# Turning the outer group's tiles of the first norm by DMA in an eight-core diffusion layer

## The chip, the cores and the metric

The kernel runs as one program on the 8 cores of a Trainium2 chip. Each core works on its own 2,048 of the 16,384 latent tokens and no core waits for another in the part that this text is about. The metric is the device time in microseconds of the slowest core.

## The reference, cut to what matters

One layer mixes windowed attention and a gated MLP over tokens, and then runs a feed-forward net. Everything that reads the input reads it through a norm and a modulation:

```
hc = modulate(layer_norm(ctx), mod_c[0], mod_c[1])      # 256 context tokens
kc, vc = context_kv(hc, w_in)
h  = modulate(layer_norm(x), mod_x[0], mod_x[1])        # latent tokens
q, k, v, u, vb, ga, gb = split(h @ w_in)
# window attention: block n reads keys and values of blocks n-1, n, n+1 and all of kc, vc
# modulate(y, shift, scale) = y * (1 + scale) + shift, shift and scale per feature
```

A core's window attention also needs the keys and values of the 128 tokens before and the 128 tokens behind its segment.

## The kernel before

The first norm writes its result with features on the partitions: `hT` holds 8 chunks of 128 features by 2,304 tokens, `hcT` the same for the 256 context tokens. The tokens come in five groups of four tiles of 128 tokens. Groups 0 to 3 are the core's own tokens; group 4, the outer group, is the tile before the segment, the tile behind it, and the two context tiles (columns 2048 to 2303 of `hT`, and all of `hcT`).

For every group the steps are: `ln_stats` (VectorE, L413 to L415), `ln_rstd` (GpSimd and VectorE, L418 to L422), `ln_norm` (ScalarE, L428: the normalised tile `xnh[i]` in bf16), `ln_turn` (TensorE, L442: 8 transposes of 128x128 per tile, into PSUM) and `ln_out` (L459 on ScalarE for chunks 0, 1, 4, 5; L463 on VectorE for chunks 2, 3, 6, 7), which reads the turned chunk from PSUM, applies scale and shift, and writes `hT` or `hcT`.

Every engine has one queue, written out in program order. The order comes from `do(seq, side)`: `seq` is a list of TensorE units (of 8 matmuls each), and `side` maps the number of a unit to work that is put behind that unit. In the stage of this change `seq` is eight units for token group 3, `u_unit` (L528) and `vb_unit` (L558) in turn. Behind a `vb_unit` the norm of the gated MLP is queued too: `vn_stats` (VectorE L570, L571; GpSimd L572, L574), and after the next unit `vn_norm` (VectorE, L581). The side work `s3` holds the norm of group 4, and also `p0_issue` and `p0_compute`: blocks of the modulation weights `wada`, 1 MB each in bf16, are loaded through GpSimd's DMA queue and used by TensorE (L349), whose result VectorE adds to (`mod_out`, L359 and L362). The last two of them, blocks 8 and 9, are `p0_compute(0)` and `p0_compute(1)` behind unit 7; they use banks 0 and 1.

Behind the eight units come, in TensorE's order: `qk_mm(4, 4)` (L488: keys of the outer tiles, bank 2; its matmul k waits for chunk k of `hT`), the context keys (L705, bank 0, which waits for all of group 4 and for what bank 0 held: the `mod_out` of block 8), `v_unit(4)` (L540: 32 matmuls, the values of the four tiles), the matmul of the rotary step (L499), and the first scores of attention (L809), which wait for the rotated keys of the outer tile (VectorE L503 and L505, GpSimd L511). Attention, the merge, the feed-forward net and the last norm follow.

SP's queue carries loads and stores. In the stage it holds the two loads of the rotary tables for group 4 (L240), and behind them nothing until the loads of `wout` at 203 us. Later in the kernel, `c2_turn` (L1039) turns the tiles of the second norm by DMA from SP's queue, and `c2_out` (L1044) modulates them in place by VectorE, 128x512 at a time.

Of the kernel before, what the change touches and what calls it, by code (L numbers as in the profile page):

```python
# [9 lines left out]
ALU = mybir.AluOpType  # L10
# [129 lines left out]
def build_nc(debug_stop=None):  # L140
    nc = bass.Bass("TRN2", target_bir_lowering=False)
    es = ExitStack()
    S = Sched()
# [68 lines left out]
    hT, _, nbA = A.alloc(BF16, [8, TH])  # L212
# [36 lines left out]
    def colpos(ti):  # L249
        return {0: 2048, NT + 1: 2176}.get(ti, (ti - 1) * 128)  # L250
# [6 lines left out]
    hcT, _, nb = A.alloc(BF16, [8, CTX], at=o); o += nb  # L257
# [13 lines left out]
    xnh = [A.alloc(BF16, [D], at=at)[0] for at in (  # L271
        RD + 16 * 1024, RD + 18 * 1024, RE_FREE + 20 * 1024, RE_FREE + 22 * 1024)]
# [5 lines left out]
    groups = [[('x', 1 + 4 * g + i) for i in range(4)] for g in range(4)]  # L278
# [46 lines left out]
    def sp_consts():  # L325
        t_gb.append(sp_load(g1bc, badabc_d[:, 0:1024], 'g1b'))
        t_gb.append(sp_load(g2bc, badabc_d[:, 1024:2048], 'g2b'))
        for dst, src in ((bsbc, bsbc_d), (esink, esink_d), (glgc, glgc_d)):
# [7 lines left out]
                 deps=[t_sc])  # L336
# [29 lines left out]
    def mcol(kind, chunk, which):  # L366
        return modc4[:, kind, chunk, which:which + 1]
# [37 lines left out]
    ln = [dict(ag=[None] * 4, xn=[None] * 4) for _ in groups]  # L405
    xnh_free = [None] * 4
    mv_free = [None] * 4
    t_hT = [[None] * 8 for _ in groups]
# [57 lines left out]
            fb_free[banks[n // 2]] = t_hT[g][c] = t_e  # L466


    qraw_free = [None, None]
    rt_free = [None, None]  # L470
    t_qg = [[] for _ in range(4)]
# [123 lines left out]
    t_mod = [[], []]  # L595
# [46 lines left out]
    def side_of(g, at, last):  # L642
        side = {}

        def put(n, *work):
            side.setdefault(min(n, last), []).extend(work)

        for i in range(4):
            if g < 4:
                put(at + i, (ln_stats, g, i))  # L650
                put(at + 4 + i, (ln_norm, g, i))
            else:
                put(at + i, (ln_norm, g, i))
            n = at + (8 if g < 4 else 4) + i
            if i:
                put(n, (ln_out, g) + PAIRS[i - 1] + (t_mod,))
            put(n, (ln_turn, g) + PAIRS[i])
        if g < 4:
            side[at + 3].append((ln_rstd, g))
        put(n + 1, (ln_out, g) + PAIRS[3] + (t_mod,))  # L660
        return side
# [10 lines left out]
    def add(side, n, *work):  # L672
        side.setdefault(n, []).extend(work)
# [21 lines left out]
        rope_load(g + 2)  # L695


    s3 = side_of(4, 0, 7)
    add(s3, 1, (p0_compute, 1), (p0_issue,))
    add(s3, 7, (p0_compute, 0), (p0_compute, 1))  # L700
    do([x_ for m in range(4) for x_ in ((u_unit, m, 3), (vb_unit, 3, m))], s3)
# [2 lines left out]
    for k in range(8):  # L704
        t_mm = S.op('pe', lambda e, k=k, pq=bk(b_)[:, 0:CTX]: e.matmul(pq, lhsT=wqk[:, 4, k, :], rhs=hcT[:, k, :],  # L705
                                                                     start=(k == 0), stop=(k == 7)),
                    deps=[fb_free[b_], t_hT[4]] if k == 0 else (), sig=(k == 7))
# [432 lines left out]
    for n, (r, tg) in enumerate(order):  # L1140
# [14 lines left out]
        if tg == 3:  # L1155
            if r + NWR < NR:
                load_w1(r + NWR)
            if r == 2:
                for i in range(2, NR):
# [4 lines left out]
                    out=scb2, in_=sc[:, 0:8].unsqueeze(2).to_broadcast([128, 8, 128])), deps=[t_wg2])  # L1164
# [239 lines left out]
```

How the kernel before makes its waits and increments, by code:

```python
            def body(engine, items=items):  # L93
                for (ws, fn, sigkey, inc) in items:
                    for (p, t) in ws:
                        engine.wait_ge(sems[p], t)
                    if fn is None:
                        continue
                    ins = fn(engine)
                    if sigkey is not None:
                        ins.then_inc(sems[sigkey], inc)
```

## Time and profile before

| | us |
|---|---|
| median of 3 runs | 980.13 (980.02 to 981.34) |
| the profiled execution's own time | 986.05 |
| span of its slowest core (core 2) | 984.4 |
| spans of the eight cores | 975.5 to 984.4 |
| TensorE busy on core 2 | 889.6 (90%) |
| VectorE, ScalarE, GpSimd busy | 482.3, 285.5, 239.2 |

The time is that of the slowest core; the profile shows one execution, and its rows are in microseconds from the start of a core's span. What one stage costs is read from the waits inside that stage, not from the busy shares of the whole.

### The profile page before, as it was taken

The numbers are of one execution on the slowest core, as the hardware profiler recorded it, in microseconds if no ns is written. First come the engines' busy times: TensorE is split into PE (matmuls) and PEld (weight loads), VectorE is DVE, ScalarE is ACT, GpSimd is POOL, SyncE is SP. The second block draws the span as 40 slices with busy tenths as digits, with TensorE's granted clock in tenths as the row PEclk, the third lists the DMA queues.
The fourth block names the chain that finished last, engine by engine and source line by source line (L and its number), as shares of the span: only waits on it lengthen the run. The fifth ranks groups of instructions, "written<-read, shape, count | busy, mean of one in ns | idle before, by whom it ended". The sixth has DMA issues, their size and how long they took to land.

```text
span 984.4 us, 15135 instructions; the slowest of 8 cores (975.5 to 984.4 us)
## 1 busy us (share of the span) xinstructions
PE 889.6 (90%) x5195; PEld 427.0 (43%) x5273; DVE 482.3 (49%) x946; ACT 285.5 (29%) x392; POOL 239.2 (24%) x282
## 2 busy tenths in 40 slices
PE   0568898889989999999998999999999999999993
PEld 0324444545544444444443444444444444444442
DVE  2147564466742366567677411122211114777774
ACT  1225545489932223332332311111111110000000
POOL 5024333266632345445443103010000000000000
PEclk9999898999999999999999999999999999999997
DMA  8999785159730023236845139962211004333231
GB/s 168 172 198 207 151 189 75 23 97 180 146 119 1 1 97 108 65 98 151 170 128 107 44 65 156 169 102 43 43 17 27 1 1 150 105 110 122 93 107 45
DMA packets 57964, 99.68 MB, mean 101 GB/s; under 512 B 20896, under 2 KB 21408, under 8 KB 57888
## 3 DMA queue, kind: packets, MB, share of 16 engines
q0 software_dynamic: 21136, 40.44, 26.4%
q1 hardware_dynamic: 36752, 58.25, 19.5%
q8 instruction: 44, 0.72, 0.3%
q14 instruction: 32, 0.26, 0.1%
HBM read 118.14 MB, written 16.78 MB: 137 GB/s over the span
## 4 chain that ended last, share of the span: by engine, by line
PE 71%; DMA 9%; DVE 6%; ACT 6%; issue 4%; POOL 1%; SPq 0%; another core or an unknown queue 0%; DVEq 0%; ACTq 0%; POOLq 0%
PE bank L1073 27%; PE bank L953 15%; PE bank L1204 14%; DMA arena<-wada 7%; ACT arena L812 4%; PE bank L984 4%; PE bank L488 2%; DMA arena<-xh 2%; PE bank L809 1%; PE bank L558 1%; PE bank L528 1%; DVE arena L1028 1%; PE bank L805 1%; PE bank L828 1%; DVE arena L1044 1%
## 5 line engine op out<-in xcount | busy, mean ns | idle before, releaser
L1073 PE MATMUL bank<-arena 128*128 128x512 bf16 x1380 | 303.8, 379 | 4.4 <-DVE arena L1084 1.9
L1073 PEld LDWEIGHTS bank<-arena 128*128 128x128 bf16 x1408 | 137.6, 98 | 169.7 <-issue 4.6
L953 PE MATMUL bank<-arena 128*128 128x512 bf16 x752 | 166.9, 379 | 2.2 <-DVE arena L969 0.9
L1084 DVE TENSOR_TENSOR arena<-bank,arena 128x512 bf16<-128x512 f32 x88 | 60.8, 692 | 217.6 <-PE bank L1073 209.5
L1204 PE MATMUL bank<-arena 128*128 128x512 bf16 (+1 forms) x734 | 151.5, 366 | 0.7
L1082 ACT ACTIVATE arena<-bank 128x512 f32<-128x512 f32 x88 | 52.2, 595 | 219.1 <-PE bank L1073 219.0
L953 PEld LDWEIGHTS bank<-arena 128*128 128x128 bf16 x768 | 74.9, 98 | 92.3 <-issue 2.7
L1204 PEld LDWEIGHTS bank<-arena 128*128 128x128 bf16 x748 | 73.2, 98 | 79.1
L969 DVE TENSOR_TENSOR arena<-bank,arena 128x512 f32<-128x512 f32 x64 | 43.2, 690 | 84.1 <-PE bank L953 65.5
L812 ACT ACTIVATE arena<-bank 128x1024 bf16<-128x1024 f32 x80 | 76.3, 1027 | 4.8 <-PE bank L809 4.5
L962 ACT ACTIVATE arena<-bank 128x512 f32<-128x512 f32 x64 | 36.7, 591 | 101.9 <-PE bank L953 101.9
L1017 ACT ACTIVATE arena<-arena 128x1024 f32<-128x1024 f32 (+1 forms) x32 | 38.5, 1235 | 81.1 <-DVE arena L1015 81.1
L984 PE MATMUL bank<-arena 128*128 128x512 bf16 x252 | 57.6, 379 | 2.7 <-DVE arena L1007 2.5
L971 POOL TENSOR_TENSOR arena<-arena 128x512 bf16<-128x512 f32 x32 | 45.1, 1409 | 57.5 <-DVE arena L969 46.1
L511 POOL TENSOR_TENSOR arena<-arena 128x512 bf16<-128x512 f32 (+1 forms) x21 | 26.0, 1240 | 89.0 <-DVE arena L505 89.0
L243 POOL DMA_DIRECT2D arena<-wff x22 | 16.4, 759 | 128.3 <-PE bank L1073 128.3
L488 PE MATMUL bank<-arena 128*128 128x512 bf16 (+1 forms) x164 | 39.5, 385 | 7.5 <-DMA arena<-wqk 3.0
L1225 ACT ACTIVATE arena<-arena 128x1 f32<-128x1 f32 x16 | 4.7, 294 | 136.3 <-DVE arena L1224 136.3
L1024 POOL TENSOR_TENSOR arena<-arena 128x1024 f32<-128x1024 f32 x16 | 37.7, 2357 | 24.4 <-ACT arena L1017 24.3
L984 PEld LDWEIGHTS bank<-arena 128*128 128x128 bf16 x256 | 24.9, 98 | 33.2 <-issue 3.4
L809 PE MATMUL bank<-arena 64*128 64x512 bf16 x160 | 31.3, 384 | 6.6 <-ACT arena L812 2.9
L442 PE MATMUL bank<-arena 128*128 128x128 bf16 x160 | 13.9, 236 | 25.0 <-ACT arena L428 24.7
(107 smaller groups left out, 869.6 us busy)
## 6 DMA issues: line engine op xcount, KB each, us to landing
arena<-xh SPq DMA_DIRECT2D x34, 512.0 KB, 6.1
arena<-wada POOLq DMA_DIRECT2D x12, 1024.0 KB, 17.2
arena<-wff POOLq DMA_DIRECT2D x11, 1024.0 KB, 10.0
xmid_d<-arena SPq DMA_DIRECT2D x16, 512.0 KB, 2.9
arena<-xmid_d SPq DMA_DIRECT2D x16, 512.0 KB, 3.8
out<-arena SPq DMA_DIRECT2D x32, 256.0 KB, 2.0
arena<-wff POOLq DMA_DIRECT2D x11, 512.0 KB, 20.0
arena<-wout SPq DMA_DIRECT2D x16, 256.0 KB, 4.5
```

Source lines behind the costliest of these rows:

```text
L488: t_mm = S.op('pe', lambda e, k=k, pq=pq, m=m, rhs=hT[:, k, g * 512:g * 512 + n_]: e.matmul(pq, lhsT=wqk[:, m, k, :], rhs=rhs, start=(k == ...
L809: t_mm = S.op('pe', lambda e, psb=bk(2 * i2 + kv), ksrc=ksrc, kv=kv, j=j, first=not masked: e.matmul(psb, lhsT=ksrc[kv * 64:(kv + 1) * 64, ...
L812: t_e = S.op('act', lambda e, pt=PT[slot], psb=bk2(2 * i2): e.activation(out=pt.rearrange('p a b -> p (a b)'), in_=psb, func=AF.Exp, scale ...
L953: t_mm = S.op('pe', lambda e, k=k, n=n, p=bk(bank), lhs=w[:, lo + k, :], rhs=src[:, k, tok]: e.matmul(p, lhsT=lhs, rhs=rhs, start=(k == 0) ...
L969: fb_free[2 + i] = t_p = S.op('dve', lambda e, dst=sga[r + i], p=bk(2 + i): e.tensor_tensor(out=dst, in0=p, in1=dst, op=ALU.mult), deps=[d ...
L971: t_merged[(m, tg)] = S.op('pool', lambda e, dst=merged[tg % 2][:, m, :], a=sga[r], b=sga[r + 1]: e.tensor_tensor(out=dst, in0=a, in1=b, o ...
L984: rhs=woutb[:, k, half * 512:(half + 1) * 512]: e.matmul(p, lhsT=lhs, rhs=rhs, start=(k == 0), stop=(k == 7)),
L1017: st_free[slot] = t2 = S.op('act', lambda e, w=w, dst=dst: e.activation(out=dst, in_=w, func=AF.Identity, scale=mv[:, 2:3], bias=mv[:, 3:4 ...
L1073: rhs=h2T[:, k, tok]: e.matmul(p, lhsT=lhs, rhs=rhs, start=(k == 0), stop=(k == 7)),
L1082: fb_free[b0] = t_s = S.op('act', lambda e, dst=sgb[s_], p=bk(b0): e.activation(out=dst, in_=p, func=AF.Silu), deps=[t_p[0], sg_free[s_]])
L1084: fb_free[b0 + 1] = sg_free[s_] = t_act[(f, tg)] = S.op('dve', lambda e, f=f, p=bk(b0 + 1), sg=sgb[s_]: e.tensor_tensor(out=act[f][:, tok] ...
L1204: t_mm = S.op('pe', lambda e, pd=bk(b_)[:, 0:cs.stop - cs.start], f=f, t=t, cs=cs: e.matmul(pd, lhsT=act[f][:, t * 128:(t + 1) * 128], rhs ...
```

## The change

The outer group no longer goes through `ln_turn` and `ln_out`. Behind each of the first four units `ln_norm` is followed by `ln_dturn`, which puts one DMA transpose of a whole 128x1024 tile on SP's queue. Behind unit 6 `ln_dmod` modulates chunks 0 to 3 in place, behind unit 7 chunks 4 to 7: two VectorE instructions of 128x256 per chunk, one in `hT` (waits for tiles 0 and 1) and one in `hcT` (waits for tiles 2 and 3). Groups 0 to 3 stay as they are.

```diff
+    def ln_dturn(i):
+        kindt, ti = groups[4][i]
+        dst = hT[:, :, colpos(ti):colpos(ti) + 128] if kindt == 'x' else hcT[:, :, ti * 128:(ti + 1) * 128]
+        ln[4][('dt', i)] = S.dma('sp', lambda e, dst=dst, src=xnh[i]: e.dma_start_transpose(out=dst, in_=src),
+                                 'hturn%d' % i, deps=[ln[4]['xn'][i]])
+
+    def ln_dmod(chunks, t_mod):
+        for c in chunks:
+            for h, which, t_d in ((hT[:, c, 2048:2304], 0, [ln[4][('dt', 0)], ln[4][('dt', 1)]]),
+                                  (hcT[:, c, :], 1, [ln[4][('dt', 2)], ln[4][('dt', 3)]])):
+                t_hT[4][c] = S.op('dve', lambda e, h=h, c=c, which=which: e.tensor_scalar(
+                    out=h, in0=h, scalar1=mcol(1, c, which), scalar2=mcol(0, c, which), op0=ALU.mult, op1=ALU.add),
+                    deps=[t_d, t_mod[c // 4]])
...
-    s3 = side_of(4, 0, 7)
+    s3 = {0: [(ln_norm, 4, 0), (ln_dturn, 0)], 1: [(ln_norm, 4, 1), (ln_dturn, 1)], 2: [(ln_norm, 4, 2), (ln_dturn, 2)],
+          3: [(ln_norm, 4, 3), (ln_dturn, 3)], 6: [(ln_dmod, (0, 1, 2, 3), t_mod)], 7: [(ln_dmod, (4, 5, 6, 7), t_mod)]}
     add(s3, 1, (p0_compute, 1), (p0_issue,))
     add(s3, 7, (p0_compute, 0), (p0_compute, 1))
```

## Rows read from the trace of the kernel before

**Rows 1.** Spans and mean granted TensorE clock of two cores.

```profile
core 2: 984.4 us, clock 0.983
core 3: 979.2 us, clock 0.980
```

**Rows 2.** Chain that ended last, core 2 (start, length, what).

```profile
161.00 16.13 DMA arena<-wada
```

**Rows 3.** Timeline of TensorE, core 2 (start, length, line, operands, count, [idle before <-releaser]).

```profile
167.33 0.68 PE L442 MATMUL bank<-arena 128*128 128x128 bf16 x8
167.85 1.89 PE L558 MATMUL bank<-arena 128*128 128x512 bf16 x8
...
177.27 0.99 PE L349 MATMUL bank<-arena 128*128 128x2 bf16 x32 [1.91 <-DMA arena<-wada]
...
179.33 1.91 PE L705 MATMUL bank<-arena 128*128 128x256 bf16 x8
181.03 2.44 PE L540 MATMUL bank<-arena 128*128 128x128 bf16 x32
183.31 0.27 PE L499 MATMUL bank<-arena 128*128 128x256 bf16 x1
185.33 0.39 PE L809 MATMUL bank<-arena 64*128 64x512 bf16 x2 [1.76 <-POOL arena L511]
```

**Rows 4.** Timeline of SP and ScalarE, core 2.

```profile
158.78 1.78 SPq L240 DMA_DIRECT2D arena<-ropes  x1
...
166.36 1.23 ACT L428 ACTIVATE arena<-arena 128x1024 bf16<-128x1024 f32 x1
```

**Rows 5.** All 16 DMA transposes of core 2 (L1039), issue to landing.

```profile
DMA to landing us min/median/max: 2.7/2.8/10.8
```

**Rows 6.** The DMA transpose issued at 455.3 us, core 2.

```profile
L1039 SPq DMA_TRANSPOSE arena<-arena x1: 1238/1238/1238, 455.3 to 455.3; - x1
...
DMA to landing us min/median/max: 10.1/10.1/10.1
```

**Rows 7.** The weight load (L243, wff) issued at 455.1 us, core 2.

```profile
DMA to landing us min/median/max: 10.0/10.0/10.0
```

**Rows 8.** Stretches of core 2 (us, length, granted clock, DMA share, GB/s).

```profile
357.50:358.50 1.00, 1.00 0.95 218
358.50:359.50 1.00, 1.00 0.21 44
...
170.00:177.00 7.00, 1.00 0.75 133
179.00:182.00 3.00, 0.50 0.02 5
```

**Rows 9.** Timeline of VectorE, core 2, in this stage.

```profile
174.88 0.69 DVE L570 BATCH_NORM_STATS2 arena<-arena 128x6 f32<-128x512 f32 x1 [0.34 <-ACT arena L562]
...
175.78 1.37 DVE L463 TENSOR_SCALAR arena<-bank,arena 128x256 bf16<-128x256 bf16 x4
...
178.36 0.17 DVE L359 TENSOR_TENSOR arena<-bank,arena 128x8 f32<-128x8 f32 x1 [0.86 <-PE bank L349]
178.64 0.17 DVE L362 TENSOR_SCALAR arena<-arena 128x8 f32<-128x8 f32 x1
```

**Rows 10.** Timeline of VectorE, core 2, modulation in place of the second norm.

```profile
554.47 2.68 DVE L1044 TENSOR_SCALAR arena<-arena 128x512 bf16<-128x512 bf16 x8
```

**Rows 11.** Timeline of TensorE, core 3.

```profile
172.19 1.84 PE L349 MATMUL bank<-arena 128*128 128x2 bf16 x64
...
175.47 1.03 PE L705 MATMUL bank<-arena 128*128 128x256 bf16 x8
...
180.16 0.39 PE L809 MATMUL bank<-arena 64*128 64x512 bf16 x2 [1.75 <-POOL arena L511]
```

**Rows 12.** The load of wada issued at 159.9 us, core 3.

```profile
L243 POOL DMA_DIRECT2D arena<-wada x1: 1006/1006/1006, 159.9 to 159.9; - x1
...
DMA to landing us min/median/max: 12.8/12.8/12.8
```

## The prediction

> **What bounds the kernel now.** I read the spans of all cores first: 975.5 to 984.4 us, core 2 the longest and core 3 nearer to the middle [rows 1]. The profiled execution took 986.05 us, 1.65 above its longest span and 5.9 above the median of the runs. So I work out a difference inside core 2, test it on core 3, and add it to the median.
>
> The page says that TensorE is busy 90% of the span. In the stage of this change the chain of waits says something else: on core 2 it runs for 16.13 us over a transfer, the load of `wada` block 9, issued at 161.00 and landed at 177.13 [rows 2]. The timeline of TensorE shows the same: it has finished all its units, waits 1.91 us for that load, and goes on at 177.27 [rows 3]. From there it is a serial chain: the keys of the outer tiles, the context keys at 179.33, the values at 181.03, the rotary step, the first scores at 185.33. After that every engine follows TensorE's order, with nothing left that waits for a clock time. So what the first scores lose, the kernel loses. I found no slack behind them that would give it back.
>
> Core 3 has the same chain without the wait: both `wada` blocks run back to back (64 matmuls in 1.84 us), the context keys start at 175.47, the first scores at 180.16 [rows 11], with the load landing at 159.9 + 12.8 = 172.7 [rows 12].
>
> **What the change removes.** 32 transposes leave TensorE. Eight of them move the next unit by 167.85 - 167.33 = 0.52 us [rows 3]; the other three blocks cost 0.45 each, 1.87 in all. On core 2 this makes TensorE wait 1.87 us longer for block 9: worth nothing. On core 3 it would be worth at most what lies between 172.19 + 0.92 (the start of the second block) and 172.7, about 0.4 us. ScalarE loses eight `ln_out` instructions, but the rest of them sits behind TensorE's units, and on core 2 nothing after them is due before block 9. Worth nothing.
>
> **What it adds on the DMA engines.** One transpose alone keeps them busy for 0.95 + 0.21 = 1.16 us [rows 8] and lands 2.8 us after its issue [rows 5]. Four are 4.64 us of engine time. The last can be issued when the fourth norm is done, at 166.36 + 1.23 = 167.6 [rows 4]. If they were alone they would land by about 171, early enough. They are not alone: from 170 to 177 the DMA engines are busy 0.75 of 7 us, that is 5.25 us of work, nearly all of it block 9 [rows 8], and ahead of the transposes SP's own queue holds the rotary tables, issued at 158.78 [rows 4].
>
> What a transpose does beside such a load is in the trace once plainly: issued at 455.3 with a 1 MB weight load issued 0.1 us before it, it landed after 10.1 us instead of 2.8, at 465.4 [rows 6]; the load landed at 465.1 [rows 7]. The transpose did not pass the load, it came out with it, although it is only 1.16 us of work. Four transposes in one queue must then come out behind it. The engines' work is conserved: block 9 lands at 177.13 with the engines otherwise free, so load and transposes together land near 177.13 + 4.64 = 181.8. A part of one transpose goes through while the load runs and while engines are idle; I take 0.5 us off: the four have landed at **181.3**. The bounds are 177.1 (all of them slip in beside the load, as fast as its tail) and, if four in one queue pay their whole 2.8 us one after another, 177.1 + 11.2 = 188.3. What keeps me near the lower half: the issue of one takes 1.24 us [rows 6], about its 1.16 of transfer, so they should follow each other closely.
>
> The Trainium skill speaks of this in "DMA: Bandwidth & Descriptors", section "Queues, rings and completion order": each DMA engine goes round robin between its queues packet by packet, a packet being several descriptors. By that the transposes might take a fair half and finish before the load; that is the third rival below. Its page "VectorE: DVE Perf Modes", section "The three transpose paths", speaks against this change more strongly: it gives 1309 ns for a 128x128 block by DMA against 390 ns by TensorE. Taken block by block, 32 blocks would be an estimated 42 us by that page and the kernel some 20 us slower still; the trace does not agree, since a whole tile of eight blocks is 1.16 us of the engines.
>
> **What it adds on VectorE.** 16 instructions of 128x256 wait at the head of VectorE's queue, behind unit 6, from about 173 on. Their price: eight of 128x512 in place start every 2.68/8 = 0.335 us [rows 10], four of 128x256 from PSUM every 1.37/4 = 0.34 [rows 9], eight columns take 0.17 (L362) [rows 9]. For 128x256 from SBUF I take the middle, 0.27 (bounds 0.17 and 0.34): 16 x 0.27 = 4.3 us (2.7 to 5.4). Before, these 16 were split over two engines and hidden in the units.
>
> Queued behind the first eight on VectorE: `vn_stats` of the last tile (174.88 to 175.78 = 0.90 with its aggregate [rows 9]), then the other eight, then `mod_out` of block 8 (178.36 to 178.64 + 0.17 = 0.45 [rows 9]). Who waits for them: `qk_mm(4, 4)` for chunk after chunk, and the context keys on bank 0 for that `mod_out`. So the context keys start at
>
> 181.3 + 4.3 + 0.9 + 0.45 + 0.05 = 187.0, where they started at 179.33: **+7.7 us**.
>
> The keys' own matmuls run in the shadow of VectorE's sixteen, and block 9's matmuls (about 1 us from 177.3) in the shadow of the transposes. If the transposes were early this cover would be gone, and that 1 us would be back on the path.
>
> **The clock.** On core 2 the granted clock was 0.50, the lower level (1.2 GHz), from 179 to 182 [rows 8], after TensorE had stood still for 1.91 us. From the context keys to the first scores core 2 took 6.00 us, core 3, which had not stood still, 180.16 - 175.47 = 4.69 [rows 3, 11]. After the change TensorE stands still, but for 1 us, from about 173.5 to 181.6, and the keys' eight matmuls come singly. I expect all of the stretch at the lower level: context keys 1.70 as in [rows 3], 32 matmuls of the values at half speed 3.4 in place of the 183.31 - 181.03 = 2.3 of [rows 3] (of which a part was at the higher level again), the rest as it is: 7.15 us, **+1.15** on core 2, +2.5 on core 3. If it were the higher level throughout, it would be -1.3 and 0.
>
> **The sum.** Core 2: +7.7 + 1.15 = +8.85 us. Core 3: transposes landed at 172.7 + 4.2 = 176.9, context keys at 176.9 + 5.7 = 182.6 against 175.47, +7.1, and +2.5 for the clock: +9.6. Both say about 9; 980.13 + 8.85 = **989.0 us**, 0.9% slower. In the profiled execution's own terms 986.05 would be 994.9.
>
> **The rivals.**
> - *The transposes land in time* (the other side). On core 2 the context keys keep their 179.33 if the four have landed by 179.33 - 5.7 = 173.6; on core 3 by 169.8. For it: undisturbed they would be there at about 171. Against it: 10.1 and 10.8 us in the two cases beside a weight load [rows 5, 6]. Where it holds, the load of block 9 remains the wait and nothing moves on core 2 (980.1); a core without the wait wins 0.4 (979.7), and all of the 1.87 us where the load is early too (978.2). Only the last is near 0.2%. Chance 0.08: 0.05 the same, 0.03 faster.
> - *Transposes one by one.* If each of the four starts only when the one before has landed, the last lands at 177.1 + 4 x 2.8 = 188.3 instead of 181.3: 7 us more, 996. Half of that, 992.5, if they overlap partly. Against it: the issue of 1.24 us. Chance 0.14.
> - *The load is the late one.* The transposes take their full turn: from about 170 on, half the engines each, landed at 170 + 2 x 4.64 = 179.3, and block 9 at 177.13 + 4.64 = 181.8, hidden behind VectorE's sixteen. Context keys at 179.3 + 5.7 = 185.0, +5.7, with the clock +6.9: 987.0. Chance 0.17.
> - *The clock comes back early*: as forecast, with 4.7 us from context keys to scores on all cores: +7.7 - 1.3 = +6.4, 986.5. Chance 0.15.
>
> **How the numbers follow.** A difference of 0.2%, about 2 us, is what a measurement of this kernel can tell from none. The forecast itself has 0.46; with its bounds (VectorE 2.7 to 5.4, half a transpose more or less) it spans 987 to 991. The rivals below it reach to 986.5, with VectorE at its lower bound to 985; the serial one in part to 992.5. The range 984.5 to 993 leaves out the case in time (0.08) and the fully serial one (0.07). Slower 0.92, the same 0.05, faster 0.03.
>
> **What would show it.** Right: four transposes at 160 to 168 us in SP's queue whose landing takes 10 us and more, the last behind block 9; VectorE idle from about 173 to 181 with its wait put down to a DMA of the arena; TensorE idle for the same time; a group of 16 instructions of 128x256 at 0.27 us each; the first scores of core 2's kind of chain some 24 us behind the issue of block 9 turned into 33. Wrong: transposes that land within 3 to 5 us, or a wait that TensorE spends for `wada` alone; then the premise that a transpose can't pass a load is what failed. If the wait is there but the loss is 2 us smaller or larger, it is the clock, or the pace of sixteen small instructions.

## The result and the profile after

The changed kernel takes 994.0 us (median of 4 runs, 992.06 to 996.17) against 980.74 for the kernel before (4 runs, 980.02 to 981.52): ratio 1.0132, 95% interval 1.012 to 1.0145. That is 1.3% slower where 0.9% was forecast, and 1.0 us outside the range. The page is of core 3, with a span of 993.0 and an own time of 994.55. Some executions of many kernels here, the one before too, have two or more cores 14 us or more longer at a granted clock of 0.96 or less, whatever the change; the medians below hold such executions, and the ratios leave most of them out.

Spans and granted clock of the changed kernel, all cores:

```profile
core 0: 989.8 us, clock 0.978
core 1: 992.1 us, clock 0.978
core 2: 986.1 us, clock 0.981
core 3: 993.0 us, clock 0.978
core 4: 987.6 us, clock 0.973
core 5: 990.5 us, clock 0.971
core 6: 986.7 us, clock 0.983
core 7: 987.6 us, clock 0.969
```

Because the cores start the stage at different times, I count from the issue of block 9 (the last L243 on `wada`). Line numbers have moved: L472 is the DMA transpose, L479 the modulation in place, L503 the outer keys, L721 the context keys, L555 the values, L825 the first scores. Core 2, the answer to [rows 2, 3, 9] (timeline):

```profile
153.98 1.62 SPq L240 DMA_DIRECT2D arena<-ropes  x1
155.70 11.85 SPq L472 DMA_TRANSPOSE arena<-arena  x2
156.20 1.00 POOL L243 DMA_DIRECT2D arena<-wada  x1
...
171.56 0.99 PE L349 MATMUL bank<-arena 128*128 128x2 bf16 x32 [2.78 <-DMA arena<-wada]
173.11 0.35 DVE L479 TENSOR_SCALAR arena<-arena 128x256 bf16<-128x256 bf16 x1 [5.08 <-DMA arena<-arena]
175.30 1.88 DVE L479 TENSOR_SCALAR arena<-arena 128x256 bf16<-128x256 bf16 x7 [1.85 <-DMA arena<-arena]
...
180.59 1.86 PE L721 MATMUL bank<-arena 128*128 128x256 bf16 x8
...
187.01 0.39 PE L825 MATMUL bank<-arena 64*128 64x512 bf16 x2 [1.76 <-POOL arena L526]
```

The same timeline of core 3, the answer to [rows 11, 12]:

```profile
153.75 0.56 SPq L240 DMA_DIRECT2D arena<-ropes  x1
154.40 15.76 SPq L472 DMA_TRANSPOSE arena<-arena  x2
155.96 1.00 POOL L243 DMA_DIRECT2D arena<-wada  x1
...
179.71 0.99 PE L349 MATMUL bank<-arena 128*128 128x2 bf16 x32 [12.60 <-DMA arena<-wada]
180.41 0.35 DVE L479 TENSOR_SCALAR arena<-arena 128x256 bf16<-128x256 bf16 x1 [14.05 <-DMA arena<-arena]
182.26 1.88 DVE L479 TENSOR_SCALAR arena<-arena 128x256 bf16<-128x256 bf16 x7 [1.51 <-DMA arena<-arena]
184.95 2.10 DVE L479 TENSOR_SCALAR arena<-arena 128x256 bf16<-128x256 bf16 x8
...
187.55 1.87 PE L721 MATMUL bank<-arena 128*128 128x256 bf16 x8
...
194.04 0.39 PE L825 MATMUL bank<-arena 64*128 64x512 bf16 x2 [1.75 <-POOL arena L526]
```

Both cores show the forecast chain: VectorE waits for a DMA of the arena, then sixteen small instructions, then the context keys. From the last landing to the context keys both take 5.5 us. What differs is the landing. TensorE waits 2.78 us for block 9 on core 2 and 12.60 on core 3. The landing of the four transposes and of block 9 on core 3:

```profile
L472 SPq DMA_TRANSPOSE arena<-arena x4: 2951/4839/12702, 154.4 to 176.8; - x4
...
DMA to landing us min/median/max: 5.2/16.9/23.0
...
L243 POOL DMA_DIRECT2D arena<-wada x1: 1004/1004/1004, 156.0 to 156.0; - x1
...
DMA to landing us min/median/max: 23.6/23.6/23.6
```

Block 9 needs 23.6 us there, against 12.8 before [rows 12] and 15.2 on core 2. The four transposes of core 2:

```profile
L472 SPq DMA_TRANSPOSE arena<-arena x4: 1237/4132/7712, 155.7 to 172.0; - x4
...
DMA to landing us min/median/max: 3.1/9.7/16.3
```

The stretches of core 3 (us, length, busy PE, PEld, DVE, ACT, POOL, granted clock, DMA share, GB/s) say that the engines were not waiting for work:

```profile
160.00:165.00 5.00, 5.00 (x25) 2.25 (x23) 2.30 (x5) 2.74 (x5) 1.01 (x3) 1.00 1.28 117
165.00:170.00 5.00, 2.12 (x38) 1.39 (x36) 0.55 (x1) 0.85 (x2) 0.57 (x1) 1.00 1.59 102
170.00:175.00 5.00, 0.00 (x0) 0.00 (x0) 0.00 (x0) 0.00 (x0) 0.00 (x0) 0.58 1.48 67
175.00:180.00 5.00, 0.29 (x11) 0.32 (x12) 0.00 (x0) 0.00 (x0) 0.00 (x0) 0.50 1.35 110
180.00:185.00 5.00, 2.19 (x31) 1.03 (x28) 2.98 (x11) 0.00 (x0) 0.00 (x0) 0.50 0.36 80
185.00:190.00 5.00, 3.92 (x20) 2.40 (x21) 3.43 (x15) 0.77 (x2) 0.88 (x2) 0.50 0.01 3
```

Core 2 moved 173 and 186 GB/s in the first two stretches at shares of 1.04 and 1.21; core 3 moved 117 and 102 at higher shares. The DMA view of 160 to 170 us tells more (queue, packets, MB, share of the 16 engines), core 3 first, then core 2; q0 carries the loads of `wada`, q1 is SP's queue with the transposes and the rest of the rotary tables:

```profile
q1 hardware_dynamic: 1165, 0.40, 79.4%
q0 software_dynamic: 355, 0.68, 63.3%
```

```profile
q0 software_dynamic: 707, 1.39, 83.3%
q1 hardware_dynamic: 822, 0.38, 28.2%
```

The shares of several queues add up, so the sum can pass 1. The mean time of one packet is the share, times 16 engines, times 10 us, over the number of packets. A packet of the load took 0.29 us on core 3 and 0.19 on core 2; one of SP's queue 0.11 and 0.055, where a transpose that is alone needs 0.018 (1056 packets, 58.1% of 2 us, core 2 before from 357.5 to 359.5). On core 3 three packets of SP's queue went for each of the load, on core 2 hardly more than one. The eight cores fall into two kinds (us from the issue of block 9):

| | before, 8 cores | after, cores 0, 2, 4, 6 | after, cores 1, 3, 5, 7 |
|---|---|---|---|
| first transpose issued | - | -0.1 to -0.5 | -1.5 to -1.6 |
| block 9 landed | 12.7 to 16.1 | 14.4 to 15.5 | 19.0 to 23.6 |
| last transpose landed | - | 18.1 to 19.3 | 21.5 to 26.1 |
| context keys | 15.2 to 18.3 | 23.6 to 24.8 | 27.0 to 31.6 |
| first scores | 19.9 to 24.3 | 30.6 to 31.0 | 33.5 to 38.1 |

From the first scores to the end all cores take 799 to 802 us, before and after, as the forecast assumed. So the loss lies wholly ahead of them, and the question is why one core of each pair (0-1, 2-3, 4-5, 6-7) sees both the load and the transposes late. I call those cores the late ones.

Where the two distances in the first row of the table come from can be read in SP's queue: it issues the first transpose right behind the load of the rotary table `ropes`. That issue takes 0.5 to 0.7 us on one core of each pair and 1.6 to 2.0 us on the other (0.56 on core 3, 1.62 on core 2, above), and in the kernel before it did so too (0.60 and 1.78). No row shows why the two cores of a pair differ in it.

### The profile page after: what moved, and what is told of

Read it like the earlier page. It is cut to its first block, busy times and chain, and to the rows that moved or that the text cites. A ratio compares the mean times of both kernels' runs of the same rounds, so it can differ in the third digit from the quotient of the medians.

```text
span 993.0 us, 15176 instructions; the slowest of 8 cores (986.1 to 993.0 us)
## 1 busy us (share of the span) xinstructions
PE 893.4 (90%) x5241; PEld 425.2 (43%) x5241; DVE 483.0 (49%) x954; ACT 281.9 (28%) x384; POOL 238.7 (24%) x282
## 3 DMA queue, kind: packets, MB, share of 16 engines
q0 software_dynamic: 21136, 40.44, 26.1%
q1 hardware_dynamic: 40976, 59.30, 21.5%
## 4 chain that ended last, share of the span: by engine, by line
PE 71%; DVE 7%; DMA 7%; ACT 5%; issue 4%; SPq 2%; POOL 2%; another core or an unknown queue 1%; DVEq 0%; ACTq 0%; POOLq 0%
PE bank L1089 27%; PE bank L969 15%; PE bank L1220 14%; DMA arena<-wqk 5%; PE bank L1000 3%; ACT arena L828 3%; PE bank L503 3%; SPq L472 2%; PE bank L825 1%; DMA arena<-wada 1%; PE bank L573 1%; PE bank L821 1%; DVE arena L1044 1%; PE bank L543 1%; PE bank L844 1%
## 5 line engine op out<-in xcount | busy, mean ns | idle before, releaser
L1089 PE MATMUL bank<-arena 128*128 128x512 bf16 x1408 | 305.5, 379 | 2.7 <-DVE arena L1100 1.9
L969 PE MATMUL bank<-arena 128*128 128x512 bf16 x768 | 167.9, 379 | 1.4 <-DVE arena L985 0.8
L1220 PE MATMUL bank<-arena 128*128 128x512 bf16 (+1 forms) x748 | 152.2, 366 | 0.0
L1000 PE MATMUL bank<-arena 128*128 128x512 bf16 x256 | 57.9, 379 | 2.3 <-DVE arena L1023 2.3
L503 PE MATMUL bank<-arena 128*128 128x512 bf16 (+1 forms) x168 | 40.8, 378 | 10.7 <-DMA arena<-wqk 3.7
L243 POOL DMA_DIRECT2D arena<-wff x22 | 16.4, 763 | 129.6 <-PE bank L1089 129.6
L1040 POOL TENSOR_TENSOR arena<-arena 128x1024 f32<-128x1024 f32 x16 | 37.7, 2357 | 24.4 <-ACT arena L1033 24.3
L825 PE MATMUL bank<-arena 64*128 64x512 bf16 x160 | 31.3, 384 | 6.0 <-ACT arena L828 2.3
L573 PE MATMUL bank<-arena 128*128 128x512 bf16 x128 | 32.8, 404 | 4.0 <-DMA arena<-wvvb 4.0
## 6 DMA issues: line engine op xcount, KB each, us to landing
arena<-wff POOLq DMA_DIRECT2D x11, 1024.0 KB, 10.6
```

The costliest lines, as they stand in the source:

```text
L503: t_mm = S.op('pe', lambda e, k=k, pq=pq, m=m, rhs=hT[:, k, g * 512:g * 512 + n_]: e.matmul(pq, lhsT=wqk[:, m, k, :], rhs=rhs, start=(k == ...
L573: t_mm = S.op('pe', lambda e, k=k, pvb=bk(b_), lh=hT[:, k, mt * 128:(mt + 1) * 128]: e.matmul(pvb, lhsT=lh, rhs=wvvb[:, k, 128:640], start ...
L825: t_mm = S.op('pe', lambda e, psb=bk(2 * i2 + kv), ksrc=ksrc, kv=kv, j=j, first=not masked: e.matmul(psb, lhsT=ksrc[kv * 64:(kv + 1) * 64, ...
L969: t_mm = S.op('pe', lambda e, k=k, n=n, p=bk(bank), lhs=w[:, lo + k, :], rhs=src[:, k, tok]: e.matmul(p, lhsT=lhs, rhs=rhs, start=(k == 0) ...
L1000: rhs=woutb[:, k, half * 512:(half + 1) * 512]: e.matmul(p, lhsT=lhs, rhs=rhs, start=(k == 0), stop=(k == 7)),
L1089: rhs=h2T[:, k, tok]: e.matmul(p, lhsT=lhs, rhs=rhs, start=(k == 0), stop=(k == 7)),
```

## The experiments

**Company without a consumer.** The kernel before, with the four transposes added at the same places, into tiles whose space is dead, read by nobody. The tiles of attention that reuse the space wait for them too, which costs nothing: the last landed 1.6 us and more ahead of the first scores on every core. The plain copy is the same bytes in the same 256-byte pieces.

```diff
...
+        S_ = lambda e, dst=dst, src=xnh[i]: e.dma_start_transpose(out=dst, in_=src)
+        t_dum[i] = S.dma('sp', S_, 'hdum%d' % i, deps=[ln[4]['xn'][i]])
...
+    for i in range(4):              # d1_turn: range(1)
+        s3[i].insert(1, (dummy, i))
# d4_copy instead of the transpose:
+        S_ = lambda e, dst=dst, src=xnh[i]: e.dma_start(out=dst, in_=src.rearrange('p (a c) -> p a c', a=8))
```

> The kernel before, with four DMA transposes of the same tiles added to SP's queue behind the four norms, into the used-up input tiles; nothing of the computation reads them, so only their traffic is added (the TensorE transposes stay). Theory A (DMA transposes that run beside a weight load make both slow, on one core of each pair): the load of block 9, 12.8 to 16.1 us from issue to landing before, takes some 15 us on four cores and 19 to 23 us on the other four; there the first scores are 4 to 8 us late and the time is 985 to 989. Theory B (the engines' work is only added up, the forecast's premise): block 9 lands at most 1 us later on every core, the transposes 4 us behind it, and the time is 980 to 982.

> As the run before, with plain copies of the same four tiles in pieces of 256 bytes (1,024 per tile) in the place of the transposes. If it is the number of small packets that slows the load (theory A1), block 9 lands as late as with the transposes, 19 to 23 us on the slow cores, time 985 to 989. If it is what is peculiar to transposes (theory A2), block 9 lands within 1 us of before and the time is 980 to 982.

> The kernel before with one added DMA transpose (of the first tile, read by nobody) in the place of four. Theory A with a loss that grows with the transposes in company: four cost the load of block 9 on the slow cores some 8 us, one costs 2 us: 981.5 to 983. A loss that comes whole with the first one: 986 to 988. None: 981.

Measured: four transposes 988.41 us, ratio 1.0067 (1.0041 to 1.0094); one transpose 987.4, 1.0058 (1.0035 to 1.0081; three of its five runs took 986.27 to 987.4); four copies 981.67, 0.9998 (0.9984 to 1.0012). Nothing is computed from the added transfers, and yet block 9 lands 22.3 to 22.8 us behind its issue on one core of each pair (1, 3, 4, 6) with four transposes, and 18.7 to 23.3 (0, 2, 5, 7) with one. On the other cores it is 14.0 to 15.0. With copies it is 13.0 to 15.7 everywhere. Core 3 with four transposes (timeline, landing), then core 4 with four copies:

```profile
153.16 24.77 SPq L703 DMA_TRANSPOSE arena<-arena  x4
154.76 1.01 POOL L243 DMA_DIRECT2D arena<-wada  x1
...
177.58 0.99 PE L349 MATMUL bank<-arena 128*128 128x2 bf16 x32 [9.78 <-DMA arena<-wada]
```

```profile
154.23 15.00 SPq L703 DMA_DIRECT2D arena<-arena  x4
155.90 1.01 POOL L243 DMA_DIRECT2D arena<-wada  x1
...
168.23 1.84 PE L349 MATMUL bank<-arena 128*128 128x2 bf16 x64
```

Both have the first transfer 1.6 to 1.7 us ahead of the load; only beside the transposes does TensorE wait 9.78 us. So it is peculiar to the transpose, and most of it comes with the first one: bytes and number of pieces are not the cause, the time of a piece is. From 160 to 168 us the copies on core 4 moved 1806 packets at 33.6% of the engines, 0.024 us each, and the load 551; the transposes on core 3 moved 657 at 87.3%, 0.17 us each, and the load 158. Which core of the pair is late changed between kernels, so it is no property of a core's number; it was each time the one with the short issue of `ropes`.

**The transposes kept until block 9 has landed.**

```diff
-                                 'hturn%d' % i, deps=[ln[4]['xn'][i]])
+                                 'hturn%d' % i, deps=[ln[4]['xn'][i], dq['issued'][-1][2]])
# all four are queued behind the fourth norm, as in late4 below
```

> The changed kernel with its four DMA transposes held back on SP's queue until block 9 of wada has landed, so that no transpose runs beside a load. Theory A: block 9 lands 12.8 to 16 us after its issue again on all cores, the transposes land 4 x 1.24 + 1.6 = 6.6 us behind it, context keys 5.4 us later: first scores 12.8 + 6.6 + 5.4 + 6.5 = 31.3 us behind the issue of block 9 in place of 30.6 to 38.1; the slow cores win, time about 990. Theory B (sum of work): the transposes lose the overlap, time 994 + 2 = 996. Rival C (transposes of the two cores of a pair hinder each other, load or not): the slow cores stay slow, their transposes land 10 us and more behind block 9, 995 or more.

Measured: 993.99 us, ratio 1.0122 (1.0096 to 1.0149). No core is late: block 9 +12.0 to 14.6, last transpose +19.3 to 22.0, context keys +24.7 to 27.5, first scores +30.6 to 34.0. About 990 was expected if only the company cost. Without company the four need 7.3 to 7.5 us behind the load, and not the 6.6 expected, twice what they need when they are queued beside it. So one disadvantage is paid for with the other.

**All four issued behind the fourth norm.** 5.2 to 6.8 us behind the load's issue.

```diff
-                                 'hturn%d' % i, deps=[ln[4]['xn'][i]])
+                                 'hturn%d' % i, deps=[ln[4]['xn'][3]])
-    s3 = {0: [(ln_norm, 4, 0), (ln_dturn, 0)], 1: [(ln_norm, 4, 1), (ln_dturn, 1)], ...
+    s3 = {0: [(ln_norm, 4, 0)], 1: [(ln_norm, 4, 1)], 2: [(ln_norm, 4, 2)],
+          3: [(ln_norm, 4, 3), (ln_dturn, 0), (ln_dturn, 1), (ln_dturn, 2), (ln_dturn, 3)], ...
```

> The changed kernel with all four transposes issued only when the fourth norm is done (some 5 us behind the issue of block 9), still beside its load. On the slow cores the first transpose was issued 1.5 us ahead of block 9, on the fast ones 0.1 to 0.5 us. Theory A (any company slows one core of each pair): again one core of each pair has block 9 landing after 19 us and more, 991 to 995. Rival (the order of issue decides, a transpose queued ahead of the load makes the loss): all eight cores are like the fast ones, block 9 after 13 to 15.5 us, last transpose 4 us later, 987 to 989.5.

> The run late4 again, for its time: in its profile no core had block 9 landing after more than 15.7 us and the last transpose after more than 19.6, so what is left should be the forecast's sum. Theory O (a transpose issued ahead of block 9 costs one core of each pair 5 to 9 us): 988 to 990 on undisturbed cores, spans 982 to 988. Theory A (any company): 992 and more, a core of each pair near 990.

The second is the same kernel again. In both profiles block 9 lands at +12.4 to 15.9, the last transpose at +16.8 to 19.8, the first scores start at +28.3 to 32.0: no late core. The medians, 1002.01 and 996.38, don't measure that: in five of nine runs a pair of cores is some 14 us longer, and in the one of them that has a profile the time goes behind the first scores (814 us to the end in place of 799). The four runs without such a pair took 988.4, 989.1, 989.6 and 989.8 us. This is the forecast's number, but these runs are a selection.

**Which comes first.** load_first issues block 9 right behind block 8, 1.8 to 3.3 us ahead of the first transpose, and to free its slot puts the matmuls of block 7 behind unit 8 of the group before; load_last issues block 9 when the third norm is done.

```diff
# load_first
+    add(s2, 8, (p0_compute, 7))
-    add(s2, 12, (ln_rstd, 4), (p0_issue,))
+    add(s2, 12, (ln_rstd, 4), (p0_issue,), (p0_issue,))
-    add(s3, 1, (p0_compute, 1), (p0_issue,))
# load_last: deps of the load of block 9
+ ln[4]['xn'][2] if blk == 9 else None
```

> The changed kernel with blocks 8 and 9 issued back to back where block 8 was, 3 us before the first transpose can be issued; the loads still run beside the transposes. Theory O: no core is slow, block 9 lands some 15 us behind its issue on all eight, the last transpose 4 us behind it; since block 9 is issued 3 us earlier the stage is 3 us shorter than in late4: 984.5 to 987. Theory A: one core of each pair keeps 5 to 9 us, 989 to 992.

> The changed kernel with block 9 issued only when the third norm is done, 3 us later than before, so that on every core two transposes are issued ahead of it. Theory O as a matter of order alone: all eight cores are slow now, block 9 lands 19 us and more behind its issue everywhere, 995 to 1000. If it is one core of each pair whatever the order, four cores are slow as before and the time is 993 to 996. If block 9 is alone with transposes and no rotary table or block 8 matters, it could land after 12 to 14 us and the time fall to 989.

load_first: 989.98 us, ratio 1.0086 (1.0057 to 1.0116), nine of its ten runs within 988.75 to 991.42. Block 9 lands +16.1 to 19.4, which is 17.0 to 20.3 us behind the issue of block 8, where the kernel before has 17.0 to 20.4 and the late cores of the changed one have 23.3 to 27.9: no late core. But block 9, issued 3.4 us sooner, did not land sooner: it still comes 5.7 to 8.0 us behind block 8. So the 3 us that were expected (984.5 to 987) did not come. load_last: 996.96, 1.0146 (1.0039 to 1.0254); the two of its four runs in which no core was over 990 took 990.04 and 991.03. In its profile transposes go 4.2 to 6.1 us ahead of the load on all cores, and yet block 9 lands at +10.6 to 13.3. "A transpose ahead of the load" is therefore not enough to make a core late.

**The distance between the two.** What the late cores had in common so far was a distance of 1.5 to 1.6 us. lag makes the transposes wait for the `vn_norm` of tile 12, lead1 and lead3 make the load wait; in these two, as in load_last, it is also queued one unit later.

```diff
# lag: deps of the transposes; lead1: the same token as a wait of the load of block 9
+ t_vn[12]
# lead3: the load of block 9 waits for the gelu of unit 2
+ t_gu[3][-1]
```

> The changed kernel with its first three transposes waiting also for the vn_norm of tile 12, which VectorE starts about 0.15 us behind the issue of block 9 and ends 0.7 us behind it: the first transpose is issued 0.8 us behind block 9 on every core, where it was issued 0.1 to 0.5 us ahead on four cores and 1.5 us ahead on the four late ones. Theory D (the distance decides: a load issued about 1.5 us behind a transpose is the one that is held back): block 9 lands 13 to 16 us behind its issue on all eight cores, the last transpose 17 to 20, the first scores 30 to 31, and the kernel takes 989 to 990 us. Theory P (one core of each pair is held back whatever the order): four cores stay at 19 to 23 us for block 9 and the time at 993 to 995.

> The changed kernel with block 9 issued only when the vn_norm of tile 12 is done, 0.75 us later than now: the first transpose is issued about 1.2 us ahead of it on the even cores and about 2.3 us ahead on the odd ones (now 0.1 to 0.5 and 1.5). Theory D: the even cores, or all eight, now see block 9 land 19 us or more behind its issue; if the distance must be near 1.5 us, the odd ones are freed (13 to 16). The time is 993 us or more if any core is held back. Theory P: as the changed kernel, one core of each pair, whatever the distance, 994.

> The changed kernel with block 9 issued when the gelu of unit 2 is done: the first transpose is issued 3 to 4 us ahead of it. Between the 1.5 us at which cores are held back and the 4.2 to 6.1 us of load_last, where block 9 landed 10.6 to 13.3 us behind its issue on all cores. Theory D: block 9 within 14 us of its issue on all eight cores, last transpose 14 to 17 us behind block 9's issue, 989 to 991 us. If any lead over 1 us holds the load back, block 9 takes 19 us or more on some cores and the time is 994 or more. Theory P: one core of each pair at 19 us or more.

lag: 990.0 us (989.76 to 991.34), ratio 1.0093 (1.0073 to 1.0112). All transposes go 0.8 to 0.9 us behind the load, and no core is late: block 9 +12.4 to 16.2, last transpose 3.5 to 3.7 us behind it on every core, first scores +27.9 to 31.4. Core 3 of lag (timeline):

```profile
155.68 1.00 POOL L243 DMA_DIRECT2D arena<-wada  x1
156.53 15.21 SPq L472 DMA_TRANSPOSE arena<-arena  x4
170.26 0.99 PE L349 MATMUL bank<-arena 128*128 128x2 bf16 x32 [3.34 <-DMA arena<-wada]
...
173.79 1.88 DVE L479 TENSOR_SCALAR arena<-arena 128x256 bf16<-128x256 bf16 x7 [1.74 <-DMA arena<-arena]
...
186.30 0.39 PE L825 MATMUL bank<-arena 64*128 64x512 bf16 x2 [1.75 <-POOL arena L526]
```

This core was the worst of the changed kernel. One wait of SP, which issues the first transpose 2.4 us later, makes its load 9 us earlier and the kernel 4 us faster (994.0 to 990.0). The theory that one core of a pair is late whatever the order falls with lag, where the issue of `ropes` still differs within each pair (0.58 us on this core), and with load_first.

lead1: 991.67 us, 1.0116 (1.0083 to 1.015). lead3: 994.42, 1.0123 (1.0071 to 1.0175). The leads came out as 1.6 to 3.0 and 2.7 to 4.9 us. In lead1 three cores with 1.6 to 1.7 were not late (12.7 to 13.8), against the expectation; of the five with 2.5 to 3.0 one was (23.6), three had 16.2 to 18.0, one 11.6. In lead3 the three cores with 2.7 to 2.9 had 16.9 to 19.0, the five with 3.8 to 4.9 had 11.3 to 14.3; the time expected for it, 989 to 991, was missed, and the slowest cores of its profile are those three. Over the changed kernel, the added transposes, lead1 and lead3, block 9 landed later than 16.2 us on 18 of the 23 cores on which a transpose was issued 1.5 to 3.0 us ahead of it. On none of the other cores profiled with transposes near the load (0.7 us ahead or less, behind it, or 3.8 us ahead and more) did it, load_first apart, where block 9 stands behind block 8. So the distance decides in the main, but not alone: the same 1.6 us was late in twelve cores of three kernels and harmless in three of lead1. Two things differ there: block 9 is issued 5.6 us behind block 8 in place of 4.3, and these three are the cores with the long issue of `ropes` (1.7 to 1.8 us), where the twelve had the short one. No run separates the two.

**The wait at the end, and the clock.** hold_warm is hold with 24 matmuls of 512 columns that compute nothing needed, ahead of the outer keys.

> The run hold (transposes held until block 9 has landed) with 24 more matmuls of 128x512 on TensorE between the matmuls of block 9 and the outer keys, into a bank that nobody reads: work only to fill the idle time. If the lower clock is what stretches context keys to first scores from 4.7 to 6.0 to 6.9 us, that falls to 4.7 to 5.2 us and the time of hold (993.99) falls by 1.5 to 2 us: 992 to 992.5. If the stretch has another cause, 994 or later.

992.25 us, 1.0144 (1.004 to 1.0248): too wide to say anything of the time. The rows do: on core 5 the granted clock was 1.00 while they ran (170 to 175 us); behind them the keys' matmuls came one by one, TensorE was busy for 2.17 of the 5 us from 175 to 180, and from 180 to 186 the clock was 0.50 again. Context keys to first scores stayed at 5.7 to 7.1 us, where 4.7 to 5.2 was expected. This filler did not buy the clock's share back.

**Blocks 8 and 9 off this place.** late_p0 (of the kernel before) puts only their matmuls behind `v_unit(4)`. moved (of the changed one) loads them behind the last transpose and computes them behind the last keys; moved_pe is the same of the kernel before.

```diff
-    add(s3, 7, (p0_compute, 0), (p0_compute, 1))
+    p0_compute(6)        # behind v_unit(4), or behind the last keys
+    p0_compute(7)
# the edits that move the two loads in moved and moved_pe are left out here
```

> The kernel before, all transposes on TensorE, with the matmuls of blocks 8 and 9 of wada moved behind the values and the rotary matmul of the outer group, on banks 6 and 7. If the wait for block 9 lies on the chain as read (1.9 us on one core, 1.6, 0.6 and 0.3 on three others, and the lower clock behind the two longest), TensorE does them in the 1.76 us in which it waits for GpSimd before the first scores: 977.5 to 979.5. If another wait ends last, 980 to 981.

> The changed kernel with the loads of blocks 8 and 9 of wada put behind the landing of the last transpose, and their matmuls behind the last keys and values of token group 3 (banks 6 and 7), so that the transposes have the DMA engines to themselves. Theory A (the loss comes from the company of the loads): the transposes land 3 us after their issue on all eight cores, 3 us behind the last norm; the sixteen VectorE instructions and the vn_stats among them take 5.2 us; context keys 8.2 us behind the last norm where they were 10.0 before on a core without a wait; time 978 to 980.5. Rival (DMA transposes of the two cores of a pair hinder each other without a load): one core of each pair stays some us late, 984 or more.

> The control of the run before it: the kernel before, transposes on TensorE, with the same move of the loads and matmuls of blocks 8 and 9. The wait for block 9 and 2 us of TensorE's work go from the stage and come back in attention, where TensorE waits for ScalarE: 978 to 980.5. If it is as fast as the run with the transposes by DMA, the change itself is worth nothing even without a collision; if slower by 1 us or more, the DMA transposes gain.

late_p0: 980.84, 0.9993 (0.998 to 1.0005), against the 977.5 to 979.5 expected. The wait for block 9 is gone on all eight cores of its profile, and the time is the same: the 1.91 us of core 2 [rows 3] were not what set the median of the kernel before. moved: 985.0, 1.0039 (1.0026 to 1.0052). moved_pe: 982.86, 1.0007 (0.9965 to 1.0049). Both missed the 978 to 980.5 expected: from the first scores to the end they take 802 to 804 us, where the kernel before has 799 to 802. In moved the transposes are in time and VectorE's sixteen start with no wait for a DMA; still the first scores come 16.7 us behind the end of the fourth norm on nearly all cores, against 14.5 on six cores and 16.1 on two in moved_pe. So even undisturbed, the change costs: the sixteen on one engine put the context keys 0.6 us later (10.4 against 9.8), and from context keys to first scores seven cores take 6.2 to 6.3 us and one 6.7, against 4.69 on the six, which is the duration of [rows 11].

**The loads 20 us earlier.** Block 8 is loaded behind unit 6 of the group before, block 9 behind unit 8; the use stays where it was.

```diff
-    add(s2, 6, (p0_compute, 6))
+    add(s2, 6, (p0_compute, 6), (p0_issue,))
+    add(s2, 8, (p0_compute, 7), (p0_issue,))
-    add(s2, 12, (ln_rstd, 4), (p0_issue,))
+    add(s2, 12, (ln_rstd, 4))
-    add(s3, 1, (p0_compute, 1), (p0_issue,))
```

early_turn does this to the changed kernel, early_pe to the kernel before. early_split also gives chunks 0, 1, 4, 5 of the modulation to ScalarE, as `ln_out` does.

> The changed kernel with blocks 8 and 9 of wada loaded some 20 us earlier (block 7 is used earlier, so that its slot comes free), which is before the norms of the outer group, and used where they were. No load runs beside the transposes any more. Theory A (the company of a load is what costs): the transposes land within 5 us of the last norm on all cores, VectorE's sixteen start when VectorE is free, context keys 10.4 us and first scores 16.7 us behind the last norm as in the run moved (14.7 before), without its longer attention stage: 981.5 to 983.5. If the loss has another cause than the loads (theory B or the pair alone), 988 or more.

> The run early_turn with the modulation in place shared again between ScalarE (chunks 0, 1, 4, 5) and VectorE (2, 3, 6, 7), as ln_out shares it. The DVE term of the forecast is then halved: eight instructions, 2.1 us, and the vn_stats; TensorE gets its chunks closer together. Context keys 8.5 to 9.5 us behind the last norm, first scores 13.5 to 15: 979 to 981, equal to the kernel before or 1 us faster.

> The control: the kernel before with the same earlier loads of blocks 8 and 9, transposes on TensorE. The wait for block 9 (on two of the eight cores of the profile 1.6 and 1.9 us, with the lower clock behind it) goes: first scores 14.7 us behind the last norm on every core. 979 to 981; at best 2 us faster than before, where the slowest core is one with the wait.

| | us | ratio to before | keys, scores behind the fourth norm |
|---|---|---|---|
| early_turn | 979.96 | 0.9987 (0.9977 to 0.9998) | 10.1 to 11.7, 17.2 to 17.9 |
| early_split | 977.79 | 0.9968 (0.9958 to 0.9977) | 9.2 to 10.9, 15.2 to 17.1 |
| early_pe | 977.56 | 0.9969 (0.9956 to 0.9983) | 10.1 to 10.8, 14.7 to 15.5 |

TensorE of early_pe, core 2, where [rows 3] have the wait of 1.91 us (timeline):

```profile
165.90 0.61 PE L442 MATMUL bank<-arena 128*128 128x128 bf16 x8
166.35 1.85 PE L349 MATMUL bank<-arena 128*128 128x2 bf16 x64
168.06 1.06 PE L488 MATMUL bank<-arena 128*128 128x256 bf16 x7
...
169.63 1.03 PE L705 MATMUL bank<-arena 128*128 128x256 bf16 x8
```

With the loads gone, four transposes take SP 5.5 to 6.4 us in all (core 2 of early_turn and early_split) and the change still costs about 2 us (ratio 0.9987 against 0.9969); with the split it is level with early_pe. Both beat the two kernels of this case by 3 us or more, and this needs no transpose by DMA.

Nor is it the wait for block 9 alone, which late_p0 took away for nothing. To free the slots, the edit also takes block 7's matmuls from behind unit 1 and puts them behind unit 8 of the group before. In the kernel before they wait 3.4 us on every core for their bank, and the profile puts this down to VectorE's rotary step (core 2, timeline):

```profile
158.58 0.99 PE L349 MATMUL bank<-arena 128*128 128x2 bf16 x32 [3.42 <-DVE arena L505]
```

In early_pe this wait is gone, and the fourth norm of the group ends 3.2 to 4.3 us behind the second on all cores, where it was 6.2 to 7.6. That is the size of the gain. load_first has the same move and gains nothing by it, as its chain is held by block 9. So the 3 us came with the two together; no run has the move of block 7 alone.

## Why the prediction was wrong

**Bound and direction: right.** The path was the load of block 9 and the chain behind it; everything lost by the first scores was lost by the kernel.

**Removed: right.** TensorE got its units done sooner and waited for the load; nothing came of it.

**Landing, 181.3: the step that failed.** Its premise was "the engines' work is conserved": load and transposes together land when the sum of their work is done. On cores 0, 2, 4, 6 it held closely in time. Block 9 landed within its old range, all transposes behind it (the first on core 2 at 155.70 + 16.3 = 172.0, block 9 at 171.4), the last 3.7 us behind it where 4.14 was worked out, and in lag so on all eight. It did not come about as told, though: the forecast had all four issued by 167.6, but SP issued the third only at 167.6 and the fourth at 172.0, when block 9 had landed. On the four late cores block 9 itself took 19.0 to 23.6 us: the engines were busy, with a share of 1.3 to 1.6 on core 3, and moved as little as 67 GB/s. The two transfers did not add up: their packets took longer beside each other, 0.29 and 0.11 us on core 3 against 0.19 and 0.055 on core 2. The metric is the slowest core, so the late ones set it. The price of this alone is measured twice: 994.0 - 990.0 = 4.0 us (lag), and 988.41 - 981.67 = 6.7 us where nothing else is lost (four transposes against four copies).

Without late cores the time comes near the forecast: lag, nine runs of load_first and the four of late4 named above take 988.4 to 991.4 us against 989.0. Part of this is luck. The sum was made for core 2, +8.85 us to the first scores; core 2 lost +6.5 (30.8 - 24.3) in the changed kernel and +7.1 in lag. Core 3's kind, for which +9.6 was worked out, lost +10.3 in lag. The wait of core 2 from which the sum started did not set the median either (late_p0).

**The third rival** had half of its mechanism on the late cores, the load being late. But it had the load at 4.64 us late, with the transposes landed before it, and gave 987. In fact load and transposes came late together. It rested on taking turns; the Trainium skill says the same ("DMA: Bandwidth & Descriptors", section "Queues, rings and completion order": round robin between queues, packet by packet). The trace does not agree that this lets four small transposes through ahead of 1 MB: on no core of the changed kernel did the last transpose land before block 9. The first did on the late cores, 2.1 to 3.4 us ahead of it. **One by one** was wrong: 3.7 us for the four behind the load, not 11.2; in hold, where they have no load beside them, 7.3 to 7.5. **In time** was wrong: it needed 173.6 on core 2, they landed at 175.1 with the load issued 4.8 us sooner than before.

**VectorE, 0.27 us each: right.** 1.88 / 7 = 0.269 and, for the second eight of core 2, 2.11 / 8 = 0.264 us. From the last landing to the context keys core 2 took 180.59 - 175.1 = 5.5 us, 5.7 forecast.

**The clock: right in kind, 0.7 us too high.** The granted clock was 0.50, the lower level, from 175 to 190 on core 3. From context keys to first scores core 2 took 187.01 - 180.59 = 6.4 us, core 3 6.5, where 7.15 was worked out. TensorE's 32 matmuls of the values took 182.25 to 184.98 = 2.7 us on core 2, not 3.4, at a mean granted clock of 0.58 from 180 to 185: a part of this stretch was at the higher level again.

**Range.** Its upper end came from the serial rival alone, taken by half. I had no row for transposes that start just ahead of a load: [rows 6, 7] show one issued just behind a load, which is the harmless order, and so it is with every transpose beside a load on the eight cores of the kernel before. One such row on one side of a distance was read as the behaviour of both.

## What to carry to other kernels

When a DMA transpose is put beside a large load, look at when each is issued, on every core: here one whole-tile transpose issued 1.5 us ahead of a 1 MB load delayed that load by 4 to 9 us on one core in two, and the same issued 0.8 us behind it delayed nothing. A queue's work can be added up only if a row shows the same kind of transfer in the same order; where it doesn't, keep the upper bound open.

Before moving work from an engine to DMA, ask what the moment is already waiting for. This one waited for a load at its end and for a PSUM bank 20 us ahead of it. Taking away the first alone gained nothing (late_p0), the loads 20 us earlier together with the matmuls that waited for the bank gained the 0.3% that the transposes could not.

## What was not expected of the hardware

A share of 1.3 to 1.6 of the DMA engines with 67 to 117 GB/s (core 3), where the other kind of core had 173 to 186 at 1.04 to 1.21: busy DMA engines are no evidence of a transfer at full rate. It comes with transposes and not with copies in 256-byte pieces. That it is one core of each pair follows the issue of the rotary table, 0.5 to 0.7 us on one and mostly 1.4 us or more on the other; no run here shows what makes that differ, why the distance between transpose and load matters so much, nor why 1.6 us of it was harmless in three cores of lead1.

The four transposes came through in 3.7 us behind the load when they had been queued beside it, and needed 7.3 to 7.5 when issued only after it had landed. Even a single transpose, whose work is 1.16 us [rows 8], cost the kernel 0.6% at the wrong moment.
